# Solver levels of an RWKV-7 chunk inverse: 32 of 64 columns moved and copied per level, U in two buffers cleared by GpSimd

## The reference

```
for each of 2 layers:
  x += 1/2 * SwiGLU_1(rms(x))
  p  = rms(x) @ W_in
  y_mla  = MLA(p)      # 8 heads, chunk-causal attention
  y_rwkv = RWKV7(p)    # 8 heads of 64, state update token by token
  x += concat(rms(y_mla)*beta_a, rms(y_rwkv)*beta_r) @ W_out
  x += 1/2 * SwiGLU_2(rms(x))
RWKV7, per head and token t:
  sa    = state @ a_t
  state = state * w_t + outer(sa, b_t) + outer(v_t, k_t)
  y_t   = state @ r_t
```

## Time and profile before

| | |
|---|---|
| median of 3 runs | 1263.22 us (1262.71 to 1263.51) |
| profiled execution | 1261.26 us |
| its span | 1259.3 us |
| mean granted TensorE clock | 0.978 |
| DVE busy | 856.7 us (68%) |
| ACT busy | 512.7 us (41%) |
| POOL busy | 21.1 us (2%) |

### The profile page before, as it was taken

The page is one execution under the profiler, slowest core; times in us unless marked ns, Lnnn a source line. Parts: engine busy times, 40 slices in busy tenths (PEclk is TensorE's granted clock), DMA queues, the critical chain, the costliest instruction groups (busy, mean ns, idle before and its releaser), DMA issues.

```text
span 1259.3 us, 27079 instructions
## 1 busy us (share of the span) xinstructions
PE 1193.3 (95%) x10736; PEld 1082.3 (86%) x10750; DVE 856.7 (68%) x1480; ACT 512.7 (41%) x767; POOL 21.1 (2%) x22
## 2 busy tenths in 40 slices
PE   7999999997998999999999999999888899999998
PEld 6999998985876789999989999989668677999998
DVE  4666667688675776666676666677868648766666
ACT  4444444632120354444454444455222214444443
POOL 0000000011000000000000000000300000000000
PEclk8999999998999999999999999999799999999999
DMA  6666666531010256666656566665210103666664
GB/s 176 201 185 185 185 190 176 139 105 51 4 35 19 84 160 187 186 184 183 183 152 185 184 186 184 189 163 152 73 38 4 51 2 101 193 185 187 184 183 134
DMA packets 243982, 174.60 MB, mean 139 GB/s; under 512 B 10354, under 2 KB 228620, under 8 KB 243916
## 3 DMA queue, kind: packets, MB, share of 16 engines
q1 hardware_dynamic: 243916, 173.64, 47.3%
HBM read 172.57 MB, written 1.05 MB: 138 GB/s over the span
## 4 chain that ended last, share of the span: by engine, by line
PE 78%; DVE 17%; issue 2%; ACT 2%; DMA 1%; SPq 0%; DVEq 0%; ACTq 0%
PE bank L1237 22%; PE bank L1238 21%; PE bank L1239 21%; PE bank L1250 7%; DVE wlo L719 3%; DVE xlo L748 1%; PE bank L1287 1%; ACT whi L536 1%; DVE work L1076 1%; PE bank L1244 1%; DVE work L946 1%; DVE root L735 1%; PE bank L1274 1%; DVE work L1105 1%; DVE root L736 1%
## 5 line engine op out<-in xcount | busy, mean ns | idle before, releaser
L719 DVE TENSOR_TENSOR wlo<-raw,whi 128x1024 fp32r<-128x1024 f32 x324 | 394.1, 1220 | 238.5 <-ACT whi L536 237.6
L1237 PE MATMUL bank<-xhi,whi 128*128 128x256 f32 x1712 | 487.8, 285 | 9.6 <-DVE xlo L748 5.4
L1238 PE MATMUL bank<-xlo,whi 128*128 128x256 f32 x1712 | 485.1, 283 | 0.0
L1239 PE MATMUL bank<-xhi,wlo 128*128 128x256 f32 x1712 | 484.9, 283 | 0.0
L536 ACT ACTIVATE whi<-raw 128x1024 fp32r<-128x1024 f32 x324 | 339.7, 1052 | 280.9 <-PE bank L1239 249.7
L1237 PEld LDWEIGHTS bank<-xhi,whi 128*128 128x128 f32 x1712 | 328.7, 192 | 16.7 <-issue 7.5
L1238 PEld LDWEIGHTS bank<-xlo,whi 128*128 128x128 f32 x1712 | 328.8, 192 | 3.1
L1239 PEld LDWEIGHTS bank<-xhi,wlo 128*128 128x128 f32 x1712 | 328.8, 192 | 0.0
L1237 PE MATMUL bank<-whi,hhi 128*128 128x512 f32 x352 | 138.7, 394 | 6.5 <-DVE hlo L834 6.5
L1238 PE MATMUL bank<-wlo,hhi 128*128 128x512 f32 x352 | 137.9, 392 | 0.0
L1239 PE MATMUL bank<-whi,hlo 128*128 128x512 f32 x352 | 137.0, 389 | 0.0
(11 more groups left out here) (211 smaller groups left out, 1089.6 us busy)
## 6 DMA issues: line engine op xcount, KB each, us to landing
raw<-in_ffn_w_gate_dram SPq DMA_DIRECT2D x88, 512.0 KB, 3.9
raw<-in_ffn_w_up_dram SPq DMA_DIRECT2D x88, 512.0 KB, 3.9
raw<-in_ffn_w_down_dram SPq DMA_DIRECT2D x88, 512.0 KB, 3.6
raw<-in_w_in_dram SPq DMA_DIRECT2D x34, 512.0 KB, 3.9
raw<-in_w_out_dram SPq DMA_DIRECT2D x16, 512.0 KB, 3.8
raw<-in_w_in_dram SPq DMA_DIRECT2D x8, 256.0 KB, 3.3
raw<-in_w_q_up_dram SPq DMA_DIRECT2D x4, 384.0 KB, 3.7
xtok<-in_x_dram SPq DMA_DIRECT2D x4, 256.0 KB, 5.3
```

The lines of the kernel that those rows point to most:

```text
L719: V_.tensor_tensor(wlo[:, b.slot, 0:width], raw[:, b.slot, 0:width], whi[:, b.slot, 0:width].bitcast(F32), ALU.subtract).then_inc(lo_ready, 1)
L1237: mm(out, hi, mhi, start=start, stop=False, **kw)
L1238: mm(out, hi, mlo, start=False, stop=False, **kw)
L1239: return mm(out, lo, mhi, start=False, stop=stop, **kw)
```

## The change

At every level the matmuls of u and t move, and write, only the columns of the even blocks of size s (32 of 64), and p moves and writes only those of the odd blocks. um multiplies only the even columns, VectorE copies only the even columns of T, ScalarE only the odd columns of P (the last level's copy to `solved` stays full). The stationary operands stay 64 columns wide. As U is now written in its even columns only and stands as stationary operand with all 64, its odd columns have to be zero. There are two U buffers, units 1 and 8, used by turns. GpSimd clears both in full after p1a, and after p{k}_{b} it clears the odd blocks of the size that the buffer will have two levels on. VectorE's um waits for these clears too (`mix_zero`). Views by `halves` and `some` have runs of s values with gaps of s.

```diff
-        tC, pC, uC = stacks(0), stacks(7), stacks(1)
+        tC, pC = stacks(0), stacks(7)
+        uC = [stacks(1), stacks(8)]
+        def halves(v, k):
+            v = v.rearrange("p g (m e s) -> p g m e s", e=2, s=1 << k)
+            return v[:, :, :, 0, :], v[:, :, :, 1, :]
+        def some(v, k, odd, g):
+            return v[:, g:g + 1, :].rearrange("p o (m e s) -> p (o m) e s", e=2, s=1 << k)[:, :, odd, :]
...
+        mix_zero = Steps(sem("mix_zero"), ["z0"] + [f"z{k}_{b}" for k in (1, 2, 3) for b in range(2)])
...
+                pool.wait_ge(mix_dve.sem, mix_dve.at(l, "p1a"))
+                pool.memset(uC[0], 0.0)
+                pool.memset(uC[1], 0.0).then_inc(mix_zero.sem, mix_zero.step("z0"))
+                for k in (1, 2, 3):
+                    for b in range(2):
+                        pool.wait_ge(mix_pe.sem, mix_pe.at(l, f"p{k}_{b}"))
+                        pool.memset(halves(uC[(k + 1) % 2][:, 8 * b:8 * b + 8, :], k + 2)[1],
+                                    0.0).then_inc(mix_zero.sem, mix_zero.step(f"z{k}_{b}"))
...
-                        dst = solved[:, 8 * b:8 * b + 8, :] if k == LEVELS else pC[:, 8 * b:8 * b + 8, :]
-                        nc.scalar.activation(dst, bank[2 + b][:].rearrange("p (g i) -> p g i", g=8),
-                                             ACT.Copy).then_inc(mix_act.sem, mix_act.step(f"pc{k}_{b}"))
+                        dst, src = pC[:, 8 * b:8 * b + 8, :], bank[2 + b][:].rearrange("p (g i) -> p g i", g=8)
+                        if k == LEVELS:
+                            dst = solved[:, 8 * b:8 * b + 8, :]
+                        else:
+                            dst, src = halves(dst, k)[1], halves(src, k)[1]
+                        nc.scalar.activation(dst, src, ACT.Copy).then_inc(mix_act.sem, mix_act.step(f"pc{k}_{b}"))
...
-                    lev = con("level")[:, 64 * (k - 1):64 * k].unsqueeze(1).to_broadcast((P, 8, C))
+                    s = 1 << k
+                    lev = con("level")[:, 64 * (k - 1):64 * k].rearrange("p (m e s) -> p m e s", e=2, s=s)[:, :, 0, :]
+                    lev = lev.unsqueeze(1).to_broadcast((P, 8, C // (2 * s), s))
...
-                        V_.tensor_tensor(eight(uC, b), bank8(4 + b), lev, ALU.mult).then_inc(mix_dve.sem, mix_dve.step(f"um{k}_{b}"))
+                        dve.wait_ge(mix_zero.sem, mix_zero.at(l, f"z{k - 2}_{b}" if k > 2 else "z0"))
+                        V_.tensor_tensor(halves(eight(uC[(k + 1) % 2], b), k)[0], halves(bank8(4 + b), k)[0], lev,
+                                         ALU.mult).then_inc(mix_dve.sem, mix_dve.step(f"um{k}_{b}"))
...
-                            V_.tensor_copy(eight(tC, b), bank8(b)).then_inc(mix_dve.sem, mix_dve.step(f"tc{k}_{b}"))
+                            V_.tensor_copy(halves(eight(tC, b), k)[0],
+                                           halves(bank8(b), k)[0]).then_inc(mix_dve.sem, mix_dve.step(f"tc{k}_{b}"))
...
-                            ins = both(bank[4 + b][:, 64 * j:64 * (j + 1)], M1[:, g, 0, :], tC[:, g, :], True,
-                                       True)
+                            ins = both(some(bank[4 + b][:].rearrange("p (g i) -> p g i", g=8), k, 0, j), M1[:, g, 0, :],
+                                       some(tC, k, 0, g), True, True)
...
-                                ins = both(bank[b][:, 64 * j:64 * (j + 1)], pC[:, g, :], uC[:, g, :], False,
+                                ins = both(some(bank[b][:].rearrange("p (g i) -> p g i", g=8), k, 0, j), pC[:, g, :],
+                                           some(uC[(k + 1) % 2], k, 0, g), False,
                                            k == LEVELS - 1, skip_group_check=True)
...
-                            ins = both(bank[2 + b][:, 64 * j:64 * (j + 1)], uC[:, g, :], pC[:, g, :], False, last,
+                            ins = both(some(bank[2 + b][:].rearrange("p (g i) -> p g i", g=8), k, 1, j), uC[(k + 1) % 2][:, g, :],
+                                       some(pC, k, 1, g), False, last,
                                        skip_group_check=True)
```

## The result

| | before | changed |
|---|---|---|
| median | 1262.97 us (1260.77 to 1263.51, 4 runs) | 1284.5 us (1282.09 to 1290.86, 4 runs) |
| profiled execution / its span | 1261.26 / 1259.3 us | 1290.86 / 1288.9 us |
| mean granted clock | 0.978 | 0.952 |

What follows compares the result with a forecast made beforehand. TensorE, busy 95% of the span, was taken as the bound. Shorter VectorE masks and copies summed to 1.30 us a layer, 2.6 for both, off the median 1263.22: 1260.6 us, range 1257.5 to 1264.5.

Steps and rivals of the forecast that it cites:

- 32 fewer moving columns uncover nothing: I take 0: Solver matmuls u, t, p at every level: the weight load already ends last, so narrowing gains 0.
- rival (C): Granted clock falls in the solver as streaming drops from 54 of 58 ns to 27: 1267.6 us; chance 9%.
- level 1: Solver's first level: t1 starts 0.27 us earlier and the T copy is in time; gain 0.42 us a layer.
- level 2: Solver's second level: TensorE is the limit, with the query/key product beside it; gain 0.
- level 3: Solver's third level: halved product and copy give 0.27 us each, 6.95 becomes 6.41; gain 0.54 us a layer.
- level 4: Solver's fourth level: um, late by 0.07 us, no longer is; gain 0.07 us a layer.
- the end: Level 5: the transposes behind the solver wait for the last um and rotation; gain 0.27 us a layer.
- Rival A: TensorE gets faster in the solver: a matmul pair falls from 58 to 27 ns, total 1248 us; chance 9%.
- Rival B: GpSimd's clears hold VectorE in the solver, at most 1.2 us in the two layers: 1261.8 us; chance 13%.
- Rival D: Strided views cost TensorE at level 1, 3.7 us a layer if its loads doubled: 1268 us; chance 7%.

Runs made afterwards that it cites:

- run 2: Kernel before with only the u, t and p matmuls narrowed to 32 moving columns; masks, copies and U as before: 1288.43 us, ratio 1.0192.
- run 1: Changed kernel with u, t and p moving and writing all 64 columns again (the wide version), rest of the change kept: 1260.32 us, ratio 0.998.
- run 8: Changed kernel plus four dummy matmuls over 512 columns of zeros ahead of u at levels 2 to 5: 1279.69 us, ratio 1.0119.
- run 3: Kernel before with u, t and p moving all 64 columns, but in the order of the strided views: 1262.1 us, ratio 0.9992.
- only u wide: Changed kernel with u at 64 moving columns, t and p at 32: 1267.06 us, ratio 1.0035.

## Why the prediction was wrong

**The step that failed** is "32 fewer moving columns uncover nothing: I take 0". In time at a given clock it is right: 29.1 ns a load wide or narrow, 5.60 us for a level. But the load covered only the time of the streaming, and the streaming had kept the clock. That rival (C) was named, with 9%, and set aside with "the loads pause nowhere in the solver for more than 1.2 us". The sentence is off as a reading, since TensorE waits 1.78 us for the first mask just ahead of level 1's t (line of the kernel before):

```profile
947.25 3.81 PEld L1250 LDWEIGHTS bank<-work 64*64 64x64 f32 x128 [1.78 <-DVE work L1067]
```

Above all it takes the presence of instructions for activity, and the stretches at 0.50 with PE and PEld busy 100% show that this can't be done. Nor do the pauses explain the fall: the changed kernel waits 1.51 us before level 1's t and 0.71 before u4, the wide one 1.51 and 0.74, and only the narrow one falls behind them. Halved streaming is enough to lose the clock (run 2), columns put back are enough to keep it (run 1), and in the traces dummy streaming keeps part of it (run 8). The price was too small as well. C took one dip, 3.5 us a layer. There were two in each layer, and against the wide version the first cost 4.6 us (up to u3, 16.31 against 11.67) and the second 7.3 (from u4, 17.66 against 10.35): 12 us over the 28.4 that the rest of the change gives. A load at half clock took 24 ns more (53.3, 128 of them from 355.74 to 362.56), where C took 29.

**Steps that held**, in the version with wide matmuls: level 1 gained 0.42 (0.42 forecast), level 2 nothing, level 3 0.53 (0.54), level 4 0.07 (0.07), the end 0.26 (0.27); 1.28 a layer, 1.30 forecast. The total of that version is 1.1 to 3.9 us under the kernel before by its interval, which holds the 2.6 forecast and can't tell it from 1 or 3; the windows of the solver carry the proof. VectorE's halved mask and copy take 0.42 each in the changed kernel, against the earlier trace rows:

```profile
347.54 0.42 DVE L1093 TENSOR_TENSOR work<-bank,cst 128x256 f32<-128x256 f32 x1 [1.44 <-PE bank L1278]
...
345.67 0.42 DVE L1099 COPY work<-bank 128x256 f32<-128x256 f32 x1 [1.44 <-PE bank L1278]
```

**Rival A** (TensorE faster) is wrong: the loads of the solver came no closer than 29 ns in any run. **Rival B** (clears hold VectorE) is wrong. VectorE's product of two SBUF tensors runs beside a clear in 1.23 us (1.22 before, without one), the small ones of level 1 keep their 0.19, and the four gain products take 3.56 us beside a clear, 3.55 before:

```profile
314.98 1.23 DVE L1030 TENSOR_TENSOR work<-work,cst 128x1024 f32<-128x1024 f32 x1
315.00 0.95 POOL L435 MEMSET work<- 128x1024 f32 x1 [27.54 <-DVE work L1027]
...
332.65 0.31 POOL L440 MEMSET work<- 128x256 f32 x1 [15.81 <-PE bank L1278]
332.72 0.19 DVE L758 TENSOR_TENSOR root<-root 128x32 f32<-128x32 f32 x1
...
348.81 3.56 DVE L1066 TENSOR_TENSOR work<-work,qkgain 128x768 f32<-128x768 f32 x4
...
350.36 0.31 POOL L440 MEMSET work<- 128x256 f32 x1 [3.42 <-PE bank L1278]
```

**Rival D** (strided views) is wrong by run 3.

**Left open.** The profiled execution of the changed kernel is 29.6 us longer in span, 8.2 more than its solvers: 2.3 before the first, 5.6 between the two, 0.4 behind the second. About 1.1 us behind each solver are its own tail: the transposes that follow still run at 0.50, and VectorE's next reciprocal starts 26.56 us behind the first solver where it started 25.41 behind it before. Another 2.5 us go between 27 and 35 us behind the first solver, where the clock is down again. The changed kernel, two stretches; then the 60 us behind both solvers of the kernel before:

```profile
369.00:372.00 3.00, 2.21 (x22) 2.04 (x19) 0.47 (x1) 0.60 (x1) 0.00 (x0) 0.50 0.00 0
399.00:402.00 3.00, 2.67 (x23) 1.91 (x23) 1.75 (x5) 0.56 (x2) 0.00 (x0) 0.50 0.30 120
```
```profile
357.46:417.46 60.00, 54.32 (x683) 42.32 (x690) 33.48 (x81) 11.16 (x39) 0.00 (x0) 1.00 0.08 28
976.23:1036.23 60.00, 54.69 (x672) 42.02 (x679) 31.57 (x70) 11.16 (x39) 0.00 (x0) 0.94 0.09 28
```

The second of these dips is not the narrow matmuls' alone: the kernel before has it too, at the same distance behind its second solver (0.94 over the 60 us, 0.50 from 1005 to 1008), and not behind its first; the changed kernel stands at 0.92 over the 60 us behind both solvers (the tail included). The kernel with wide matmuls (1.00 behind both in its trace) varies from 1254 to 1264 us, at clocks of 0.977 to 0.985. What sets it off is open, and so is the rest of the 8.2 us.

## What to carry to other kernels

A weight load that ends last hides the time of the matmul behind it, not the matmul's part in keeping TensorE's clock: before narrowing a matmul that is bound by its load, take the gain as nothing and ask what the clock does. Keep matmuls full where their width is free, and take the narrowing on the engines that read the result: here that half is worth 2.5 us, the other cost 24. When PE is busy 100% at a granted clock of 0.50, the busy column is no evidence against a clock fall; look at PEclk by windows.

## What had not been expected of the hardware

- The clock fell to 0.50 with TensorE and its loads busy 9.00 of 9.00 us and 15.00 of 15.00; in the longer stretch every matmul of the solver had 32 moving columns behind a 64-column load, and the shorter one ends in the 64 transposes of v. The Trainium skill (TensorE: Matmul & The Clock Gate, "Part 1") describes the gate as following how busy TensorE has been and warns of idle gaps; these runs had the fall behind waits of 1.51 and 0.71 us that the wide kernel has too (1.51 and 0.74) without a fall, and it stayed down with no gap at all.
- Identical instructions kept the clock in one solver and lost it in the other (28.42 and 31.53 us, only u wide).
- A GpSimd clear costs a VectorE product of two SBUF tensors nothing (1.23 us), where a GpSimd product of two tensors held one of 4 elements for 2.19 us. A clear of 1024 float32 takes 0.95 us, one of 256 in runs of 8 to 32 takes 0.31.
- Float32 matmuls that read and write in runs of two values keep the 29 ns a load of contiguous ones.
